# A two-layer diffusion block on one core: the order of the gate stage in layer 0, and the last expert's output by halves of its columns

## The reference

```python
def merge_branches(p, y_s, w_four, w_glu_a, w_glu_b, w_out):
    g_a = jax.nn.sigmoid(p[..., OFF_GA:OFF_GB])
    g_b = jax.nn.sigmoid(p[..., OFF_GB:])
    y_a = fourier_mix(p[..., :OFF_SSM]) @ w_four
    y_b = (y_s @ w_glu_a) * jax.nn.sigmoid(y_s @ w_glu_b)
    return (g_a * y_a + g_b * y_b) @ w_out
...
    for e in range(N_EXPERTS):
        out = out + combine[:, e:e + 1] * swiglu(tok, w_gate[e], w_up[e], w_down[e])
...
    return rmsnorm(h, final_g)
```

## Time and profile before

| | |
|---|---|
| runs | 2034.87, 2035.4, 2527.94 us; median 2035.4 |
| the profiled execution | 2034.36 us, its span 2032.6 us |
| TensorE matmuls | 1982.9 us busy, 98% of the span |
| VectorE | 1535.1 us, 76% |
| ScalarE | 962.4 us, 47% |
| chain of waits that ended last | TensorE 89%, VectorE 7%, ScalarE 1%, DMA 1% |
| ScalarE's copies into WH (half a tile each) | 336 |
| mean granted TensorE clock | 0.996 of full |

### The profile page before, as it was taken

One profiled execution on the slowest core, in us unless ns is written; L12 is line 12 of the kernel. 1 busy time (PEld: TensorE's weight loads), 2 busy tenths in 40 slices (PEclk: granted clock), 3 DMA queues, 4 the chain that ended last, 5 costly groups with the idle time before them and its releaser, 6 DMA issues.

```text
span 2032.6 us, 24902 instructions
## 1 busy us (share of the span) xinstructions
PE 1982.9 (98%) x10214; PEld 1556.2 (77%) x10214; DVE 1535.1 (76%) x2009; ACT 962.4 (47%) x885; POOL 0.2 (0%) x4
## 2 busy tenths in 40 slices
PE   6999999999999999999999999999999999999998
PEld 3545774577788778889878888888888888888886
DVE  7788537777755774480588898888989898898986
ACT  2312212322212222411267766777767777677775
POOL 0000000000000000000000000000000000000000
PEclk9999999999999999999999999999999999999999
DMA  9345675324533443585279999899998999899994
GB/s 401 103 164 172 162 258 204 117 83 181 186 146 150 179 163 135 162 212 187 84 296 378 365 366 372 331 368 359 373 353 339 373 355 375 337 366 369 355 368 173
DMA packets 83841, 529.29 MB, mean 260 GB/s; under 512 B 23056, under 2 KB 49552, under 8 KB 52752
## 3 DMA queue, kind: packets, MB, share of 16 engines
q1 hardware_dynamic: 62976, 508.65, 67.5%
q10 hardware_dynamic: 20752, 19.05, 2.7%
HBM read 509.39 MB, written 18.28 MB: 260 GB/s over the span
## 4 chain that ended last, share of the span: by engine, by line
PE 89%; DVE 7%; ACT 1%; DMA 1%; issue 1%; ACTq 1%; SPq 0%; DVEq 0%
PE ps L2490 15%; PE ps L2475 15%; PE ps L2476 15%; PE ps L1948 10%; PE ps L1957 6%; PE ps L1964 6%; PE ps L1961 6%; PE ps L2285 1%; PE ps L2124 1%; PE ps L2419 1%; DMA ring<-in_w_mod 1%; PE ps L2230 1%; DVE H L1596 1%; DVE sc L1594 1%; PE ps L2293 1%
## 5 line engine op out<-in xcount | busy, mean ns | idle before, releaser
L1771 DVE TENSOR_TENSOR WL<-mring,WH 128x2048 fp32r<-128x2048 f32 x336 | 755.1, 2288 | 102.3 <-ACT WH L1085 102.1
L1085 ACT ACTIVATE WH<-mring 128x2048 fp32r<-128x2048 f32 x336 | 626.2, 1913 | 144.1 <-PE ps L2490 107.4
L2475 PE MATMUL ps<-WH,XGh 128*128 128x512 f32 x896 | 353.8, 395 | 0.2 <-issue 0.2
L2476 PE MATMUL ps<-WH,XGl 128*128 128x512 f32 x896 | 349.4, 390 | 0.0
L2490 PE MATMUL ps<-WL,XGh 128*128 128x512 f32 x896 | 221.6, 389 | 0.0
L2490 PEld LDWEIGHTS ps<-WL,XGh 128*128 128x128 f32 x896 | 168.2, 188 | 34.9
L2475 PEld LDWEIGHTS ps<-WH,XGh 128*128 128x128 f32 x896 | 168.3, 188 | 33.9 <-issue 0.3
L2476 PEld LDWEIGHTS ps<-WH,XGl 128*128 128x128 f32 x896 | 168.4, 188 | 33.4
L2475 PE MATMUL ps<-WH,hTh 128*128 128x512 f32 x448 | 175.8, 392 | 0.0
L2476 PE MATMUL ps<-WH,hTl 128*128 128x512 f32 x448 | 174.5, 390 | 0.0
L869 ACT ACTIVATE FWH<-ring 128x4096 fp32r<-128x4096 f32 (+2 forms) x21 | 67.9, 3233 | 217.8 <-DMA ring<-in_ffn_gu 126.9
(11 more groups left out here) (370 smaller groups left out, 2498.2 us busy)
## 6 DMA issues: line engine op xcount, KB each, us to landing
mring<-in_moe_gate SPq DMA_DIRECT2D x56, 2048.0 KB, 9.4
mring<-in_moe_up SPq DMA_DIRECT2D x56, 2048.0 KB, 9.6
mring<-in_moe_down SPq DMA_DIRECT2D x56, 2048.0 KB, 9.1
ring<-in_w_mod SPq DMA_DIRECT2D x23, 2048.0 KB, 8.1
ring<-in_w_in SPq DMA_DIRECT2D x11, 2048.0 KB, 11.5
ring<-in_ffn_gu SPq DMA_DIRECT2D x11, 2048.0 KB, 8.0
ring<-cks SPq DMA_DIRECT2D x4, 2048.0 KB, 11.2
ring<-in_w_out SPq DMA_DIRECT2D x4, 2048.0 KB, 8.3
```

The costliest lines, as they stand in the source:

```text
L1085: nc.scalar.activation(WH[buf][:, o], mring[t % MRING][:, o], ACT.Copy).then_inc(high_done, 1)
L1771: V.tensor_tensor(WL[buf][:, o], mring[t % MRING][:, o], WH[buf][:, o].bitcast(F32), ALU.subtract).then_inc(low_done, 1)
L2475: mm(out_, ah, WH[buf][:, o:o + 512], start=(first and q == 0), stop=False)
L2476: mm(out_, al, WH[buf][:, o:o + 512], start=False, stop=False)
```

## The change

Three lists of work are put in another order, and the tail is split. The arithmetic is the same.

In the gate stage ScalarE issues the load of layer 1's raw tables before `gate_high(1)` and no longer after block 0's copy. VectorE does `mod_columns(1)`, `gate_low(2)`, `powers(1)`, `tables(1)`, and then `gate_low(3)`; `in_powers(1, 0)` comes next, with `gate_low(4)` to `(6)` behind it. On TensorE turn 0 follows block 4 (it followed block 3), turn 1 follows block 6 (block 5); turn 2 stays behind block 7. ScalarE's `turned` moves with them.

In the tail, the last expert's last tile is done by `last_outputs`: all 12 matmuls of half 0 first, signalled by a new semaphore, then the 12 of half 1. ScalarE loads its table for the root, then makes `yeh` for half 0 and, after the tile, for half 1; VectorE does the same with `yel`. Both now have these behind their branch. The scatter of columns 0 to 511 waits for the first `yel` only. In the second pass, each expert's outputs are made at the start of the next one; that pass's code changes too.

```diff
--- before.py
+++ after.py
@@ -561,6 +561,7 @@
         hid_ready = sem("hid_ready")
         ye_ready = sem("ye_ready")
         ye_low = sem("ye_low")
+        first_half = sem("first_half")
 
         block = top.enter_context(nc.Block())
 
@@ -984,6 +985,9 @@
                         evac(("ga", l, m), G[:, m, t0:NT], ACT.Sigmoid, n)
                 if l == 0:
                     mod_rows(8)
+                    act.wait_ge(c_made, ITS)
+                    act.wait_ge(b_masked, 2 * ITS)
+                    act.dma_start(raw[:].rearrange("p a r c h -> p (a r c h)"), a["bc"][1]).then_inc(raw_in, 16)
                     gate_high(1)
                 for m in range(8):
                     if l == 0 and m == 3:
@@ -994,14 +998,11 @@
                         gate_high(m + 2)
                     if l == 0 and m == 2:
                         store_lags(0, 1)
-                    if l == 0 and m == 0:
-                        act.wait_ge(c_made, ITS)
-                        act.wait_ge(b_masked, 2 * ITS)
-                        act.dma_start(raw[:].rearrange("p a r c h -> p (a r c h)"), a["bc"][1]).then_inc(raw_in, 16)
-                    if l == 0 and m == 3:
+                    if l == 0 and m == 4:
                         turned(1, 0)
                     if l == 0 and m == 5:
                         mod_rows(9)
+                    if l == 0 and m == 6:
                         turned(1, 1)
                 if l == 0:
                     turned(1, 2)
@@ -1106,11 +1107,21 @@
                 take_weights(pas, "before", 0, 0)
                 split(1, 1, NE * pas)
 
+            def outputs_high(h, par):
+                nc.scalar.activation(yeh[:, 512 * h:512 * h + 512], ps[:, 4 + h, :], ACT.Copy,
+                                     scale=wslot[:, par:par + 1]).then_inc(ye_ready, 1)
+
             def pair(pas, i):
                 for par in range(2):
                     e = i * 2 + par
                     x = e + NE * pas
+                    if pas:
+                        act.wait_ge(tile_done, x * TILES)
+                        for h in range(2):
+                            outputs_high(h, 1 - par)
                     for t, (kind, c) in enumerate(moe_order):
+                        if (kind, c) == ("down", 6) and at_end(pas, i, par):
+                            continue
                         act.wait_ge(tile_done, x * TILES + t + 1)
                         if kind == "gate":
                             if c >= 2:
@@ -1132,10 +1143,9 @@
                         if (kind, c, par) == ("down", 5, 1) and not at_end(pas, i, par):
                             for g in range(2, 4):
                                 take_high(pas, i, ("G", g), xg_high(g), par)
-                        if (kind, c) == ("down", 6):
+                        if (kind, c) == ("down", 6) and not pas:
                             for h in range(2):
-                                nc.scalar.activation(yeh[:, 512 * h:512 * h + 512], ps[:, 4 + h, :], ACT.Copy,
-                                                     scale=wslot[:, par:par + 1]).then_inc(ye_ready, 1)
+                                outputs_high(h, par)
                         if t + 2 < TILES or not at_end(pas, i, par):
                             split(t + 2, (par + t) % 2, x)
 
@@ -1146,7 +1156,12 @@
             with act.If(most > P):
                 begin(1)
                 pairs_of(act, 1, lambda i: pair(1, i))
+                act.wait_ge(tile_done, 2 * NE * TILES)
             nc.scalar.activation(wt[:, 0, 1:2], epst[:], ACT.Sqrt)
+            act.wait_ge(first_half, 1)
+            outputs_high(0, 1)
+            act.wait_ge(tile_done, NE * TILES)
+            outputs_high(1, 1)
             for m in range(KD):
                 act.wait_ge(last_added, m + 1)
                 nc.scalar.activation(fin[:, m, :], hT[:, m, CTX:NT], ACT.Square).then_inc(last_squared, 1)
@@ -1606,17 +1621,16 @@
                     gate_low(0)
                     gate_low(1)
                     lag_rows(0, 1)
+                    mod_columns(1)
                     gate_low(2)
-                    mod_columns(1)
+                    powers(1)
+                    tables(1)
                     gate_low(3)
-                    powers(1)
-                    gate_low(4)
-                    tables(1)
                     for k in range(4):
                         in_powers(1, k)
                         if k == 0:
-                            gate_low(5)
-                            gate_low(6)
+                            for m in range(4, 7):
+                                gate_low(m)
                         if k == 1:
                             gate_low(7)
                 for m in range(8):
@@ -1793,11 +1807,20 @@
                 split(0, 0, NE * pas)
                 split(1, 1, NE * pas)
 
+            def outputs_low(h, par):
+                V.scalar_tensor_tensor(yel[:, 512 * h:512 * h + 512], ps[:, 4 + h, :], wslot[:, par:par + 1],
+                                       yeh[:, 512 * h:512 * h + 512].bitcast(F32),
+                                       ALU.mult, ALU.subtract).then_inc(ye_low, 1)
+
             def pair(pas, i):
                 for par in range(2):
                     e = i * 2 + par
                     x = e + NE * pas
                     head = pas == 0 and (i, par) == (0, 0)
+                    if pas:
+                        for h in range(2):
+                            dve.wait_ge(ye_ready, x * 2 + h - 1)
+                            outputs_low(h, 1 - par)
                     for t, (kind, c) in enumerate(moe_order):
                         if kind == "gate" and c >= 1:
                             take_low(pas, i, ("T", c - 1), ht(hTh, c - 1), ht(hTl, c - 1), par)
@@ -1829,13 +1852,10 @@
                         if (kind, c, par) == ("down", 5, 1) and not at_end(pas, i, par):
                             for g in range(2, 4):
                                 take_low(pas, i, ("G", g), xg(XGh, g), xg(XGl, g), par)
-                        if (kind, c) == ("down", 6):
+                        if (kind, c) == ("down", 6) and not pas and not at_end(pas, i, par):
                             for h in range(2):
                                 dve.wait_ge(ye_ready, x * 2 + h + 1)
-                                V.scalar_tensor_tensor(yel[:, 512 * h:512 * h + 512], ps[:, 4 + h, :],
-                                                       wslot[:, par:par + 1],
-                                                       yeh[:, 512 * h:512 * h + 512].bitcast(F32),
-                                                       ALU.mult, ALU.subtract).then_inc(ye_low, 1)
+                                outputs_low(h, par)
                         if t + 2 < TILES or not at_end(pas, i, par):
                             split(t + 2, (par + t) % 2, x)
 
@@ -1846,7 +1866,10 @@
             with dve.If(most > P):
                 begin(1)
                 pairs_of(dve, 1, lambda i: pair(1, i))
-
+                dve.wait_ge(ye_ready, 4 * NE)
+            for h in range(2):
+                dve.wait_ge(ye_ready, 2 * NE - 1 + h)
+                outputs_low(h, 1)
             for m in range(KD):
                 if m % 2 == 0:
                     dve.wait_ge(last_done, m // 2 + 1)
@@ -2257,10 +2280,11 @@
                                 split_gate(4 * h + m)
                             if l == 0 and h + m == 0:
                                 lags(0, 7)
-                            if l == 0 and (h, m) == (0, 3):
+                            if l == 0 and (h, m) == (1, 0):
                                 turn(1, 0)
                             if l == 0 and (h, m) == (1, 1):
                                 mod_sums(9)
+                            if l == 0 and (h, m) == (1, 2):
                                 turn(1, 1)
                 if l == 0:
                     turn(1, 2)
@@ -2444,6 +2468,18 @@
                     b, n, _ = misc_use(pas, i, ("G", g), par)
                     pe.wait_ge(misc_taken[b], n + 1)
 
+            def last_outputs(outs, wh, wl, high):
+
+                pe.wait_ge(high_done, high + 2)
+                for h, (out_, pairs, _, _) in enumerate(outs):
+                    for (ah, al), o in pairs:
+                        mm(out_, ah, wh[:, o:o + 512], start=False, stop=False)
+                        mm(out_, al, wh[:, o:o + 512], start=False, stop=False)
+                    pe.wait_ge(low_done, high + 2)
+                    for q, ((ah, _), o) in enumerate(pairs):
+                        last = mm(out_, ah, wl[:, o:o + 512], start=False, stop=(q == len(pairs) - 1))
+                    last.then_inc(first_half if h == 0 else tile_done, 1)
+
             def pair(pas, i):
                 for par in range(2):
                     e = i * 2 + par
@@ -2465,6 +2501,9 @@
                                       for k in range(KD)], True, True)]
                             if kind == "gate" and c >= 2:
```

(6 more changed lines are left out.)

## The result

The changed kernel takes 2052.99 us (2052.45 to 2055.17, four runs) against 2035.56 for the kernel before: a ratio of 1.0089, with a 95% interval of 1.0069 to 1.0109. It is **17.4 us slower**, far outside the forecast range of 2029 to 2038. Its profiled execution took 2052.98 us, with a span of 2050.1 us and a mean granted clock of 0.986 (before: 0.996).

What follows compares the result with a forecast made beforehand. TensorE, busy for 98% of the span, was taken as the bound. Gate stage -0.15, low clock +1.5 and tail -2.8 sum to -1.45 us; from the median 2035.4 that gave 2034.0 us, range 2029.0 to 2038.0.

Steps and rivals of the forecast that it cites:

- the stall removed: Before layer 1's first turn, TensorE's wait for VectorE's BP and the low clock behind it go: 6.20 us gained.
- What is late next: At keep_on ahead of Y, TensorE waits for turn 1's store, landing at 258.0; of 6.20 us, 0.15 is left.
- At an absolute time: Turn 1's store waits until SyncE's gds loads have drained, at a time that doesn't move; landing at 258.0.
- a rival worth 9 us: Turn 1's store shares the DMA engines with the loads and lands by 252.5: full 9.0 us gain, 2026.4, chance 0.13.
- the price of the low clock: After the idle stretch before keep_on, TensorE restarts at the low clock: 1.5 us lost, between 0.5 and 3.0.
- From Y on ... nothing there is priced: From Y on, loads, turns and stores follow events on TensorE and shift with it; no cost was given.
- start at the low clock: At keep_on, after idling from 252.3 to 259.25, TensorE must restart at the low clock: 1.5 us.
- the tail: At the last tile, half 0 is finished early and VectorE's adds start at 2017.8 instead of 2020.58: 2.8 us gained.
- The slower one: At turn 2's copies, the store meets ck1 from its first packet and lands at 260.0: +2.05 us, 2037.5, chance 0.17.
- served beside the loads: Turn 1's store alternates packets with SyncE's loads and hardly delays turn 2's copies: 2026.4, chance 0.13.
- the tail did overlap: Answers a rival at the tail: ScalarE's or TensorE's branch shows, about 1 of 2.8 us left: 2035.8, chance 0.10.

Runs made afterwards that it cites:

- the run with one load: The changed kernel with seven of SyncE's eight small-packet Toeplitz loads in layer 0 left out: 2027.50 us, ratio 0.9946.
- the version with the turns back: The changed kernel with turns 0 and 1 behind blocks 3 and 5 again, the rest of the change kept: 2028.45 us, ratio 0.9947.
- the run with 10 of them: The changed kernel with keep_on of 10 instead of 2 at the head of Y, behind the wait: 2033.06 us, ratio 0.9978.
- the tail alone: The kernel before with only the change's tail edits, on its old gate stage: 2034.83 us, ratio 0.9984.
- the gate stage alone: The kernel before with only the change's gate-stage edits, early raw-table load included, and its old tail: 2054.48 us, ratio 1.0075.

## Why the prediction was wrong

**Right: the stall removed.** 6.20 us were forecast up to turn 2, 6.37 measured. Turn 0 no longer waits, and VectorE's order held: tables before gate_low(3), one in_powers after it.

**What is late next: the place right, the size off.** The wait moved to the store of turn 1, behind the small loads, and TensorE met it at keep_on; the run with one load confirms the cause. The store was issued at 249.77, on the clock of the kernel before 246.5 (246.65 forecast). But it landed at 257.57, on that clock 254.3, where I had 258.0 and a floor of 255.95. It took 7.8 us from issue and not 9.3. The wait was 3.4 us and not 7, and keep_on came 3.87 us early (2.50 of the 6.37 given back), not 0.15. Two steps of the reasoning didn't hold. "At an absolute time" is refuted by the version with the turns back, whose store was issued 5.2 us sooner and landed 4.4 us sooner, at 253.2, with small packets still to come. And ck1's load, which I had let delay the store, had little effect: from its first packets to its landing the store took 3.6 us, 254.0 to 257.6, as it had before, 253.0 to 256.6. Why the time from issue to landing varies, 7.1 to 9.5 us over the traces that have all eight loads, stays open.

The rule of the Trainium skill that a DMA engine goes round-robin between the queue rows it has work for (the Trainium skill, DMA: Bandwidth & Descriptors, Queues, rings and completion order) had been weighed as a rival worth 9 us. The trace of the changed kernel doesn't agree with it for the first 4 us of this store: 1314 packets to 4. That the version with the turns back gains just those 9.0 us is by another way: its store is issued sooner.

**Wrong: the price of the low clock, "I take 1.5 us", with 3.0 as its end, and with it "From Y on ... nothing there is priced".** That term measured 21.0 us (19.12 in Y, 1.86 until turn 4). I priced it by the low stretch that the stall before had the earlier trace rows, which lasted 3.4 us; dense work stood behind it, matmuls of 128 and 512 columns. I didn't ask what follows here. Behind keep_on come 320 matmuls of 64 columns. In the four traces with a low clock in Y they did 40 us of unbroken work and more without raising it. In two of these, both of the changed kernel, Y had even begun at the full clock and lost it after some 0.5 us; so TensorE didn't "start at the low clock", as I had it, but got it shortly afterwards. In the other eight traces, where the wait ahead was 0.89 us or had dense matmuls in it or behind it, Y kept the full clock throughout. Which property of Y's matmuls matters, their 64 columns or the 64 rows that the first lot uses, was not tested. By the size of that one term the sum goes from -1.45 to +18.1, with keep_on's real time (-3.7) to +14.3; the other 3.3 us of the profiled pair are the first line of the table.

The Trainium skill (TensorE: Matmul & The Clock Gate, Part 1: The HAM clock gate) says that the default state is throttled and that activity releases the throttle. The trace agrees for keep_on's matmuls in the run with 10 of them, 0.50 until 260.9 and 1.00 behind it. For Y's it doesn't, if a busy engine is what "activity" means: TensorE is busy for 39.60 of 39.60 us and stays at 0.50.

**Right: the tail.** 2.8 us forecast, 2.85 in the traces and 2.5 in the medians of the tail alone (1.2 to 5.5 by the interval). The rows that answer to the earlier trace rows:

```profile
2035.15 0.67 ACT L1111 ACTIVATE yeh<-ps,wslot 128x512 fp32r<-128x512 f32 x1
2036.73 0.69 ACT L1111 ACTIVATE yeh<-ps,wslot 128x512 fp32r<-128x512 f32 x1 [0.91 <-PE ps L2480]
```

```profile
2037.45 0.75 DVE L1811 SCALAR_TENSOR_TENSOR yel<-ps,wslot,yeh 128x512 fp32r<-128x512 f32 x1 [0.84 <-ACT yeh L1111]
2038.12 3.22 DVE L1877 SCALAR_TENSOR_TENSOR hT<-ps,modv,hT 128x256 f32<-128x256 f32 x8
```

```profile
L2560 PEldq COMPARE_BRANCH  x1: 3692/3692/3692, 2032.5 to 2032.5; - x1
```

ScalarE begins half 1 at 2036.73, just behind the last tile, and VectorE adds 1.4 us later, against 4.2 before. TensorE's branch, 3.69 us, again ran behind queued matmuls. One thing came close: ScalarE began half 0 only at 2035.15, more than 1 us after its 12 matmuls, since its branch and table load stood ahead of it; 0.9 us more and it would have been on the path. On the clock of the kernel before it was made at 2015.4, between the 2014.5 forecast and the 2015.7 for a branch twice as long.

**The rivals.** The slower one named the right place, an idle stretch at keep_on and then the low clock, and gave it 3.0 us; its price was wrong by the same term, and its own cause, a store held up by ck1 until 260.0, didn't come about. The store wasn't served beside the loads either, and the tail did overlap.

## What to carry to other kernels

Before you price an idle gap of TensorE, look at what runs behind it. If that is a stage of small matmuls, the gap may leave the whole stage at 1.2 GHz: here 3.4 us of idle time cost 21 on top. A few dense matmuls in the gap (8 keep_on: some 20 us won) or right behind it are cheap insurance, sized by the trace of one of them. And when a producer has been made early enough by itself, don't also move its consumer later: everything that the consumer issues, here a store that a buffer waits for, moves with it.

## What the runs showed of the hardware that was not expected

- The same 320 matmuls of Y took 22.0 us at 1.00 in eight traces and 41 to 42 us at 0.50 in four (of three kernels), TensorE being busy throughout in both. Once the clock was low they didn't raise it.
- The clock need not fall while TensorE is idle. In the changed kernel it fell some 1.6 us after TensorE had started again, in both traces; with a wait of 7.8 us, and in the gate stage alone with one of 4.15 us, it fell within the wait.
- The drop is likely, not certain: one execution in ten of the gate stage alone kept a mean clock of 0.997 and took 2034.86 us, against 2051 to 2060; all eight of the changed kernel were slow.
- A store of 512 KB on ScalarE's queue moved 4 packets in 4 us while 1314 small ones of SyncE's queue went through.
- TensorE's branch at the end of the first pass took 3.52 and 3.69 us, and cost nothing, since it ran ahead of the matmuls still queued. ScalarE's table load came 3.73 us after its last copy ("issue"); part of that is no branch, since ScalarE first waits for tile 19, whose matmuls end at 2031.2, and 2.5 us are left for it, against 1.33 before.
